# First layer of a two-block transformer: x's tiles turned ahead, another order of VectorE's splits, later small transfers, wider sums, and a joined forget product

## The reference

```
c_act = silu(c)
shift, scale, gate = split(c_act @ mod_w[i] + mod_b[i], 3)
h = rms_norm(x, norm_g[i]) * (1 + scale) + shift
layer 0: y = retention(h);  q, k, v, g = split(h @ ret_w_in)
layer 1: y = forgetting_attention(h);  q, k, v, g, f = split(h @ fox_w_in)
         log_f = log_sigmoid(f + b_f)          # f: 16 heads
x = x + gate * y
```

## Time and profile before

| what | value |
|---|---|
| median of 3 runs | 694.55 us (694.49 to 694.74) |
| the profiled execution's own time | 694.77 us |
| its span | 693.0 us |
| PE busy | 679.8 us, 98% |
| DVE busy | 502.2 us, 72% |
| ACT busy | 380.4 us, 55% |
| granted TensorE clock, mean | 0.998 of 2.4 GHz |
| DMA in slices 2 to 4 of 40 (17 to 69 us) | 368 to 391 GB/s; mean 200 |

### The profile page before, as it was taken

One profiled execution on the slowest core, in us unless ns is written; L12 is line 12 of the kernel. 1 busy time (PEld: TensorE's weight loads), 2 busy tenths in 40 slices (PEclk: granted clock), 3 DMA queues, 4 the chain that ended last, 5 costly groups with the idle time before them and its releaser, 6 DMA issues.

```text
span 693.0 us, 11560 instructions
## 1 busy us (share of the span) xinstructions
PE 679.8 (98%) x4590; PEld 554.2 (80%) x4591; DVE 502.2 (72%) x803; ACT 380.4 (55%) x561; POOL 16.3 (2%) x35
## 2 busy tenths in 40 slices
PE   8899999999999999999999999999999999999996
PEld 4679997777878888878788877778888888888885
DVE  6888988787986779766768889777665555565445
ACT  5457434565555665654655765845574444444444
POOL 4010000000000000000000000000000000000000
PEclk9999999999999999999999999999999999999999
DMA  9999785667896176833455654434656666655511
GB/s 295 368 377 391 272 265 174 201 223 230 303 339 213 51 245 225 274 128 106 135 157 158 190 164 137 139 122 120 212 156 212 182 190 178 197 185 189 186 61 61
DMA packets 74405, 138.81 MB, mean 200 GB/s; under 512 B 5732, under 2 KB 18400, under 8 KB 74352
## 3 DMA queue, kind: packets, MB, share of 16 engines
q1 hardware_dynamic: 72816, 134.92, 60.1%
q10 hardware_dynamic: 736, 1.81, 0.7%
q0 software_dynamic: 800, 1.35, 0.6%
HBM read 137.01 MB, written 1.05 MB: 199 GB/s over the span
## 4 chain that ended last, share of the span: by engine, by line
PE 90%; DVE 3%; SPq 2%; DMA 1%; ACT 1%; issue 1%; DVEq 0%; ACTq 0%
PE G L392 23%; PE G L394 22%; PE G L393 22%; PE T L433 5%; PE G L412 2%; PE G L413 2%; PE G L414 2%; PE T L791 2%; DMA arena<-in_mod_w_dram 1%; PE T L779 1%; DVE wlo L1119 1%; SPq L2547 1%; PE G L529 1%; PE G L531 1%; PE G L530 1%
## 5 line engine op out<-in xcount | busy, mean ns | idle before, releaser
L1119 DVE TENSOR_TENSOR wlo<-raw,whi 128x1024 fp32r<-128x1024 f32 x202 | 245.6, 1222 | 111.3 <-ACT whi L1927 110.9
L1927 ACT ACTIVATE whi<-raw 128x1024 fp32r<-128x1024 f32 x202 | 211.9, 1060 | 133.4 <-PE G L394 89.5
L392 PE MATMUL G<-whi,ahi 128*128 128x512 f32 x694 | 280.4, 404 | 0.2 <-DVE wlo L1119 0.2
L394 PE MATMUL G<-whi,alo 128*128 128x512 f32 x694 | 271.1, 391 | 0.0
L393 PE MATMUL G<-wlo,ahi 128*128 128x512 f32 x694 | 270.4, 390 | 0.0
L392 PEld LDWEIGHTS G<-whi,ahi 128*128 128x128 f32 x694 | 130.3, 188 | 29.3 <-issue 1.8
L394 PEld LDWEIGHTS G<-whi,alo 128*128 128x128 f32 x694 | 130.3, 188 | 28.4
L393 PEld LDWEIGHTS G<-wlo,ahi 128*128 128x128 f32 x694 | 130.6, 188 | 25.3 <-issue 1.0
L1929 ACT ACTIVATE arena<-T,st 128x128 f32<-128x128 f32 (+2 forms) x56 | 21.8, 476 | 30.0 <-DVE st L1520 30.0
L1927 ACT ACTIVATE ahi<-T 128x512 fp32r<-128x512 f32 x25 | 14.9, 597 | 39.6 <-PE T L433 39.6
L1929 ACT ACT_TABLE_LOAD x27 | 34.6, 1283 | 3.3 <-issue 1.8
(11 more groups left out here) (254 smaller groups left out, 628.8 us busy)
## 6 DMA issues: line engine op xcount, KB each, us to landing
raw<-in_ret_w_in_dram SPq DMA_DIRECT2D x48, 512.0 KB, 6.2
raw<-in_w_gate_up_dram SPq DMA_DIRECT2D x40, 512.0 KB, 4.0
raw<-in_mod_w_dram SPq DMA_DIRECT2D x32, 512.0 KB, 4.7
raw<-in_fox_w_in_dram SPq DMA_DIRECT2D x32, 512.0 KB, 4.6
raw<-in_w_in_dram SPq DMA_DIRECT2D x28, 512.0 KB, 3.7
raw<-in_w_down_dram SPq DMA_DIRECT2D x22, 512.0 KB, 3.5
arena<-in_mod_w_dram SPq DMA_DIRECT2D x16, 512.0 KB, 9.6
raw<-in_ret_w_out_dram SPq DMA_DIRECT2D x16, 512.0 KB, 5.1
```

The costliest lines, as they stand in the source:

```text
L392: e.matmul(o, ah, wh, start=first and k == 0, stop=False)
L394: done = e.matmul(o, al, wh, start=False, stop=last and k == 1)
L1119: e.tensor_tensor(o, a, b, op).then_inc(sig[name], 1)
L1927: d = e.activation(o, a, f, scale=scale)
```

## The change

Six edits.

1. **Tiles 2 to 7 are turned ahead.** `turn_two` turns two tiles at once, k = 2 and 3 before the sums of group 1, k = 4 to 7 after the products of tile 0, into T0, T1 and T0 again. ACT copies each pair from PSUM to `xT` in SBUF (`x0_copy`, 128x512, three times), and `x0_high` of tiles 2 to 7 reads `xT`. PE waits for the last copy once, before T0 and T1 take products. The sums of tile 1 move from banks T0 and T1 to T2 and T3. `xT` lies where the table `dec` is loaded later, and that load waits for `x0` at 8.
2. **Splits of a second weight unit stand between those of x.** On ACT, for k in 2, 4, 6, the next unit's high part comes between `x0_high(k)` and `x0_high(k + 1)`; on DVE its low part between `x0_low(k)` and `x0_low(k + 1)`.
3. **DVE's first step of groups 3 and 4** stands ahead of the low part of the unit before.
4. **POOL's small transfers** wait for `macc` at 5 (the last group's sum on DVE) instead of `mod0` at 12.
5. **The sums of groups 0 and 1** are 128 columns wide: 8 instructions where 32 were, and 2 where 8 were.
6. **Forget.** High and low parts of f's columns lie side by side, 32 columns per tile, so that `ahi` is multiplied once by both; the two halves (16 rows each) are added by the product that replaces the transpose, with a 0/1 matrix from the constants.

```diff
+        xT = region(11776, 1536).rearrange("p (k n) -> p k n", k=6)
+        def copied(k):
+            return 4 + k // 2
         def sums_at(k, a):
-            return (G[a] if k == 0 else T[a] if k == 1 else T[2 + k % 2])[:, 256 + 32 * a:256 + 32 * a + 32]
+            return (G[a] if k == 0 else T[2 + a] if k == 1 else T[2 + k % 2])[:, 256 + 32 * a:256 + 32 * a + 32]
...
-        zT = PTf[0:16, 0, 0:S]
+        zT = PTf[0:32, 0, 0:S]
+        narrow = ahi[:, 29, :].rearrange("p (k t n) -> p k t n", t=2, n=16)
...
             def turn_x0(k):
-                on_.wait_ge(sig["xn"], 2 if k < 4 else 4)
-                on_.wait_ge(sig["h_in"], k - 1)
-                transposes(T[2 + k % 2], [xn0[:, m, k * P:(k + 1) * P] for m in range(2)], "x0_turned")
+                on_.wait_ge(sig["xn"], 2)
+                transposes(T[2 + k], [xn0[:, m, k * P:(k + 1) * P] for m in range(2)], "x0_turned")
+            def turn_two(k):
+                on_.wait_ge(sig["xn"], 4 if k < 6 else copied(2))
+                transposes(T[k // 2 % 2 ^ 1], [xn0[:, m, k_ * P:(k_ + 1) * P] for k_ in (k, k + 1) for m in range(2)], "x0_turned")
             def own_rows(g, i, a):
-                r0 = VECTOR_ROWS[g]
+                r0, w = VECTOR_ROWS[g], P if g < 2 else 32
                 o = sums_at(SUMMED[g][i], a)
                 for r in range(r0, 8):
-                    for c in range(0, P, 32):
-                        e.matmul(o[c:c + 32, :], mod_tile(g)[:, a, r, i * P + c:i * P + c + 32], cact[:, r:r + 1].to_broadcast([P, 32]), start=r == r0, stop=False)
+                    for c in range(0, P, w):
+                        e.matmul(o[c:c + w, :], mod_tile(g)[:, a, r, i * P + c:i * P + c + w], cact[:, r:r + 1].to_broadcast([P, 32]), start=r == r0, stop=False)
...
             first_sums(0, turn_rows)
             keep_warm(6)
             rows_unit(0, 0, (0,))
+            on_.wait_ge(sig["cact"], 1)
+            turn_two(2)
             on_.wait_ge(sig["rows_read"], 3)
+            on_.wait_ge(sig["h_in"], 1)
             first_sums(1)
             rows_unit(0, 0, (1,))
+            turn_two(4)
+            turn_two(6)
             for k in range(0, 8, 2):
...
-                if k < 6:
-                    turn_x0(k + 2)
-                    turn_x0(k + 3)
+                if k == 0:
+                    on_.wait_ge(sig["xn"], copied(6))
                 products(u + 2, 0, (4, 5, None), k, k == 0, k == 6)
...
             def turn_forget():
                 on_.wait_ge(sig["forget"], 1)
+                on_.wait_ge(sig["head2_in"], 32)
                 t = bank("forget_t", sig["forget"], 2)
                 for m in range(2):
-                    d = e.transpose(t[:, 16 * m:16 * m + 16], zT[:, m * P:(m + 1) * P], idf[0:16, 0:16])
+                    d = e.matmul(t[:, 16 * m:16 * m + 16], zT[:, m * P:(m + 1) * P], head[0:32, C_SEL:C_SEL + 16], start=True, stop=True)
...
-                e.matmul(t[0:16, 0:S], wh, ahi[:, k, :], start=k == 0, stop=False)
-                e.matmul(t[0:16, 0:S], wl, ahi[:, k, :], start=False, stop=False)
-                d = e.matmul(t[0:16, 0:S], wh, alo[:, k, :], start=False, stop=k == 7)
+                e.matmul(t[0:32, 0:S], ahi[:, 29, 32 * k:32 * k + 32], ahi[:, k, :], start=k == 0, stop=False)
+                d = e.matmul(t[0:16, 0:S], narrow[:, k, 0, :], alo[:, k, :], start=False, stop=k == 7)
...
             for g in (2, 3, 4):
                 k, u = 2 * g - 2, 3 * g - 3
+                if g > 2:
+                    mod_sums(g, 0, 1)
                 ring_to(u - 1)
-                mod_sums(g, 0, 4)
+                mod_sums(g, g > 2, 4)
                 mod_sums(g, 4, VECTOR_ROWS[g])
                 modulated(k)
                 modulated(k + 1)
                 ring_to(u)
                 x0_low(k)
+                ring_to(u + 1)
                 x0_low(k + 1)
-                ring_to(u + 1)
...
+            def x0_copy(k):
+                on_.wait_ge(sig["x0_turned"], 2 + k // 2)
+                act(xT[:, k - 2:k, :], T[k // 2 % 2 ^ 1][:, :].rearrange("p (k n) -> p k n", k=2), ACT.Copy, "xn")
...
             x0_high(0)
             normal(4)
+            x0_copy(2)
             ring_to(1)
             x0_high(1)
             ring_to(2)
+            x0_copy(4)
+            x0_copy(6)
             for k in (2, 4, 6):
                 ring_to(3 * k // 2)
                 x0_high(k)
+                ring_to(3 * k // 2 + 1)
                 x0_high(k + 1)
                 ring_to(3 * k // 2 + 2)
...
-            on_.wait_ge(sig["mod0"], 12)
+            on_.wait_ge(sig["macc"], 5)
             e.dma_start(posi, pos_in.partition_broadcast(P).rearrange("p a n -> p (a n)")).then_inc(sig["small_in"], 16)
```

More of the change, by code:

```diff
@@ L466, in turn_x0 @@
             def turn_x0(k):
-                on_.wait_ge(sig["xn"], 2 if k < 4 else 4)
-                on_.wait_ge(sig["h_in"], k - 1)
-                transposes(T[2 + k % 2], [xn0[:, m, k * P:(k + 1) * P] for m in range(2)], "x0_turned")
+                on_.wait_ge(sig["xn"], 2)
[3 more added lines that the diff above has]
+                transposes(T[k // 2 % 2 ^ 1], [xn0[:, m, k_ * P:(k_ + 1) * P] for k_ in (k, k + 1) for m in range(2)], "x0_turned")
             def own_rows(g, i, a):
-                r0 = VECTOR_ROWS[g]
+                r0, w = VECTOR_ROWS[g], P if g < 2 else 32
                 o = sums_at(SUMMED[g][i], a)
                 for r in range(r0, 8):
-                    for c in range(0, P, 32):
-                        e.matmul(o[c:c + 32, :], mod_tile(g)[:, a, r, i * P + c:i * P + c + 32], cact[:, r:r + 1].to_broadcast([P, 32]), start=r == r0, stop=False)
+                    for c in range(0, P, w):
+                        e.matmul(o[c:c + w, :], mod_tile(g)[:, a, r, i * P + c:i * P + c + w], cact[:, r:r + 1].to_broadcast([P, 32]), start=r == r0, stop=False)
             def other_rows(g, i, a):
                 on_.wait_ge(sig["macc"], g + 1)
-                for c in range(0, P, 32):
-                    d = e.matmul(sums_at(SUMMED[g][i], a)[c:c + 32, :], macc[:, g % 2, a, i * P + c:i * P + c + 32], ones[:, 0:32], start=False, stop=True)
+                w = P if g < 2 else 32
+                for c in range(0, P, w):
+                    d = e.matmul(sums_at(SUMMED[g][i], a)[c:c + w, :], macc[:, g % 2, a, i * P + c:i * P + c + w], ones[:, 0:32], start=False, stop=True)
                 return d
@@ L725, in _ @@
             t = bank("forget", sig["forget"], 1)
-            nhi, nlo = ahi[:, 29, 0:P], ahi[:, 29, P:2 * P]
             for k in range(8):
@@ L729, in _ @@
                 on_.wait_ge(*ready[k, 1])
-                wh, wl = nhi[:, k * 16:(k + 1) * 16], nlo[:, k * 16:(k + 1) * 16]
-                e.matmul(t[0:16, 0:S], wh, ahi[:, k, :], start=k == 0, stop=False)
-                e.matmul(t[0:16, 0:S], wl, ahi[:, k, :], start=False, stop=False)
-                d = e.matmul(t[0:16, 0:S], wh, alo[:, k, :], start=False, stop=k == 7)
+                e.matmul(t[0:32, 0:S], ahi[:, 29, 32 * k:32 * k + 32], ahi[:, k, :], start=k == 0, stop=False)
+                d = e.matmul(t[0:16, 0:S], narrow[:, k, 0, :], alo[:, k, :], start=False, stop=k == 7)
             d.then_inc(sig["forget_pe"], 1)
@@ L1143, in item @@
                     on_.wait_ge(sig["narrow_hi"], 1)
-                    tt(ahi[:, 29, P:2 * P], raw_tile(n), ahi[:, 29, 0:P].bitcast(F32), ALU.subtract, "used")
+                    tt(narrow[:, :, 1, :], raw_tile(n).rearrange("p (k n) -> p k n", n=16), narrow[:, :, 0, :].bitcast(F32), ALU.subtract, "used")
                     return
@@ L1488, in _ @@
                     on_.wait_ge(sig["forget_pe"], 1)
-                    copy(zT, T[bank_of["forget"]][0:16, 0:S], "forget")
+                    copy(zT, T[bank_of["forget"]][0:32, 0:S], "forget")
                 head_norm(2 * c)
@@ L1944, in ring_to @@
                     if items[n][0] == "f":
-                        act(ahi[:, 29, 0:P], raw_tile(n), ACT.Copy, "narrow_hi")
+                        act(narrow[:, :, 0, :], raw_tile(n).rearrange("p (k n) -> p k n", n=16), ACT.Copy, "narrow_hi")
                         continue
@@ L2003, in x0_high @@
             def x0_high(k):
-                on_.wait_ge(sig["x0_turned"], k + 1)
+                if k < 2:
+                    on_.wait_ge(sig["x0_turned"], k + 1)
                 on_.wait_ge(sig["mod0"], 2 * k + 2)
                 on_.wait_ge(sig["x0"], k - 3)
-                act(stage0[:, k % 4, :], T[2 + k % 2][:, 0:256], ACT.Identity, "h_in", scale=col(AB[:, 0, :], k), bias=col(AB[:, 0, :], 8 + k))
+                if k >= 2:
+                    on_.wait_ge(sig["xn"], copied(k))
+                act(stage0[:, k % 4, :], T[2 + k][:, 0:256] if k < 2 else xT[:, k - 2, :], ACT.Identity, "h_in", scale=col(AB[:, 0, :], k), bias=col(AB[:, 0, :], 8 + k))
                 on_.wait_ge(sig["h_in"], k + 1)
                 act(ahi[:, k, :], stage0[:, k % 4, :], ACT.Copy, "h_hi")
+            def x0_copy(k):
```

(3 more changed lines are left out.)

## The result

The changed kernel takes 696.83 us (median of 11 runs), the kernel before 694.74 beside it: 2.1 us slower. One far longer run of each (754.65 us at a mean granted clock of 0.848, and 977.55 us) counts in these two medians; without such runs, which are left out from here on, they are 696.62 and 694.65, and the ratio of the means is 1.003, 95% interval 1.002 to 1.0039. The forecast was 694.8, its range ended at 696.0. The ten runs lie between 695.21 and 697.97 and so spread over 2.8 us, those of the kernel before over 0.7.

A forecast was written before the change was run, and what follows sets the result against it. PE was taken to bound the kernel, busy 679.8 of 693.0 us. First layer 0, bias +1.0 and forget -0.7 gave +0.3 on 694.77, so 695.07; the median lies 0.22 lower, forecast 694.8, range 692.9 to 696.0.

The forecast's parts named there:

- Bias (+1.0): DVE's first modulation item waits about 2.5 us for POOL's later bias transfer; 1.45 absorbed, PE 1.0 us later before unit 16.
- Forget (-0.7): In the forget, eight products fewer save 0.91 us and the float32 turn costs 0.22 more: net -0.7 us.
- First layer (0): Wide sums bring group 2's sum 1.3 us late, DVE's new order wins it back: 0, bounds -0.3 to +1.3.
- The wide sums are not won back: Rival, chance 0.11: the first layer's 1.3 us stay lost, PE 2.3 late at unit 16, total +1.6, 696.2 us.
- The bias lands in time: Rival, chance 0.28: POOL's bias transfer causes DVE no delay, first layer 0 to -0.3, forget -0.7: 693.7 us.
- Forget saves nothing: Rival, chance 0.05: in the forget each wide weight costs double, leaving the bias's +1.0: 695.6 us.
- Turning ahead pays in full: Rival, chance 0.10: first-layer PE stops halve and transposes go, about -2.9, with forget -0.7 and no bias wait: 691.0 us.

The follow-up runs named there:

- after_again: The changed kernel run again without any edit: median 696.62 us, ratio 1.0027 against the kernel before; its profiled execution took 695.55 us.
- look1: The changed kernel as it is, one single profiled execution: 695.65 us.
- look4: The changed kernel as it is, another single profiled execution: 695.12 us.
- look3: The changed kernel as it is, another single profiled execution: 698.21 us.
- look5: The changed kernel as it is, another single profiled execution: 698.24 us.
- b_pool: The kernel before with only POOL's five small transfers moved to wait for the fifth macc sum: 696.00 us, ratio 1.0022.
- a_wide_g1: The changed kernel with group 0's sums narrow again and group 1's still wide: 694.81 us, ratio 1.0002.
- g1_pool: The changed kernel with group 0's sums narrow, group 1's wide, and POOL's small transfers back at their old place: 693.90 us, ratio 0.9989.
- a_wide1: The changed kernel with one sum of group 2 wide as well: 695.18 us, ratio 1.0013.
- a_pool_look: The changed kernel with POOL's five small transfers back at their old place, one single profiled execution: 697.90 us.
- a_again240: The changed kernel with 240 more PE instructions, small matmuls issued again in group 2's first sum: 696.24 us, ratio 1.0027.
- b_again32: The kernel before with 32 more PE instructions, eight small matmuls issued again ahead of group 2's macc sums: 698.52 us, ratio 1.0052.

## Why the prediction was wrong

- **Bias (+1.0): right.** 2.46 us of wait forecast as 2.5, unit 16 1.02 us later, +1.2 on the median with this edit alone; in the changed kernel it shows in the four profiled executions without a stop (2.28 to 3.43 us). The first profile hid it, since a stop had made DVE nearly as late as the bias. That the size came out so close is partly luck, since two errors of about 1 us cancelled: in `after_again` POOL issued the second row 3.33 us after it went on, not 2.40, and it landed in 5.1, not 6.3.
- **Forget (-0.7): right in kind, too large.** The products gave 0.87 of 0.91, but the turn cost 0.32 instead of 0.22; alone it measures -0.45.
- **First layer (0): right as long as PE does not stop.** PE's first product behind group 4's sums and its wait for DVE's low part, before, in look1, then in look4:

```profile
50.72 0.47 PE L529 MATMUL G<-whi,ahi 128*128 128x512 f32 x1 [0.41 <-DVE alo L1119]
```

```profile
50.50 0.47 PE L541 MATMUL G<-whi,ahi 128*128 128x512 f32 x1 [0.50 <-DVE alo L1133]
```

```profile
51.16 0.47 PE L541 MATMUL G<-whi,ahi 128*128 128x512 f32 x1 [0.51 <-DVE alo L1133]
```

That is -0.2 and +0.4 us, inside -0.3 to +1.3: the 1.3 us lost at group 2 (1.6 in the first profile) are won back, as reckoned. The 0.66 us between the two are the half clock.
- **The step that failed** is "So I expect PE to be level again at the end of the first layer: 0, with bounds of -0.3 us ... and +1.3". Its bounds counted what each PE instruction lasts at full clock. It did not count that PE's instructions themselves must arrive: 240 fewer of them put other work at the borders of the blocks of 256, where the packet of the next block starts late while the DMA share is 1.0 or more. In the first profile the end of the first layer is at 52.86, 2.1 us later than before: against look1's 50.50 a stop of 1.70, 0.54 of half clock and 0.1 more. In look3 and look5 it is at 54.69 and 54.55, with stops of 1.84 and 1.03, and of 1.88 and 1.04. In 15 of 26 executions of the changed kernel the time is above 696.1; three of these were profiled, and they are the three with stops. The other 11, from 695.12 to 696.04, are what the sum gives with its terms as measured: 694.8 + 1.2 - 0.45 = 695.5.
- **The rivals.** "The wide sums are not won back" had 696.2, near the median, but its mechanism does not hold: where PE does not stop, the end of the first layer is 0.2 us earlier to 0.6 later than before, and the 1.3 us are won back. That its number came near is luck. "The bias lands in time" (693.7) falls with the wait of 2.46 us in `b_pool`, and "Forget saves nothing" (695.6) with the products' 1.85 us instead of 2.72. "Turning ahead pays in full" (691.0) was no case: in look1, without any stop for nothing, the end of the first layer is 0.2 us earlier, not 2.9.
- The Trainium skill, Runtime: NRT & Kernel Launch, section Instruction fetch mechanics, says that instructions are refilled in blocks of 16 KiB, 256 instructions, with the next block fetched while the current one runs, and that a crossing is mostly hidden. The counts 705 and 961 and the packet's 16,384 bytes agree. Hidden the crossing is at 37 of the 48 borders counted above; at the other eleven, whose packets start while the DMA share is 1.0 or more, the traces show stops of 0.8 to 2.7 us.

What is not settled: what delays the packet; why none of the 22 runs of `a_wide_g1` and `g1_pool` is a long one (the longest has 695.45); and whether every run above 696.1 has a stop, since only the profiled ones were seen. The long one of `a_wide1` had two stretches at half clock and no stop, and all 15 executions of the changed kernel above 696.1 have a mean granted clock of 0.997 or less, while the six at 0.999 or more end at 695.84. Whether the early stretch helps to make the packet late is open too; it is not needed for a stop, since `a_pool_look`, `a_again240` and `b_again32` stop without one ahead of it.

## What to carry to other kernels

Where one engine issues hundreds of short instructions while the DMA engines are full, ask when its next 256 instructions arrive: here eight matmuls more cost 3.7 us, some 1.5 of them by the half clock behind the stop. It shows as a wide spread of the times and as an idle gap for nothing at records 256 apart. Read several executions before a difference of 2 us is explained by one profile. And a transfer that is put off needs its landing time written beside its first reader: here 2.5 us of wait, as worked out.

## What the runs showed that I had not expected

- PE stops for its own instructions: 0.8 to 2.7 us, at records 705, 961 and 1217 alone, give or take one, all in the first 56 us. It goes on 2.4 to 2.6 us behind the start of the packet.
- 32 instructions that only wait for semaphores long met took 3.2 us on PE, 0.1 each, in a place where PE waited only 1.0 us before.
- The granted clock fell to 0.50 (1.2 of 2.4 GHz) at 12.6 to 13.1 us behind sixteen wide weight loads with 32 columns streaming each, in five of seven executions of the changed kernel, and behind stops (`b_again32` at 32.1, `a_pool_look` at 41.4). Its cost shows in the products: 0.66 us in look4 against look1, hidden there by the wait for the bias, and 1.5 us in `b_again32`.
